# Per-tile routing in a mixture-of-experts step: selection, ranking and expert lists made as each tile's logits arrive

## The chip, the cores and the metric

The kernel runs on one core of a Trainium2 chip. The metric is the time of one execution on the device in microseconds (us), the median of three runs. All tensors are float32.

## What is computed

A prompt of 512 rows and 8 sample rows of width 1024 pass through one decoder layer: three mixers side by side (a short convolution, a gated MLP over chunks, forgetting attention), an output projection with residual add, and then the part that is changed, a hierarchical mixture of experts with 4 groups of 8 experts:

```python
def hier_moe(h, w_grp, b_grp, w_rt, b_rt, w_gate, w_up, w_down):
    grp_prob = softmax(h @ w_grp + b_grp)
    p_g, g_idx = top_k(grp_prob, 1)
    exp_logits = (h @ w_rt + b_rt) of that group
    p_e, e_idx = top_k(softmax(exp_logits), TOP_K)      # TOP_K = 2
    w = p_g * p_e / sum(p_e)
    # per expert e: act = silu(h @ w_gate[e]) * (h @ w_up[e]) * gate;  y += act @ w_down[e]
x = x + hier_moe(rmsnorm(x, g_ffn), ...)
x = x + (p_i @ w_ple) * sigmoid(rmsnorm(x, g_ple) @ w_ple_gate)
```

A final RMSNorm follows. Each row uses 2 of 32 experts; each expert has three matrices of 2 MB (1024x512, 1024x512, 512x1024).

## The kernel before, in words

The 520 rows are five tiles: tiles 0 to 3 have 128 prompt rows each, tile 4 (`QT`) has the 8 sample rows. The five engines run instruction streams written out by hand; they meet at semaphores, and each engine takes its own instructions strictly in the order written. `step(...)` on DVE issues an instruction and waits for its end; `tell(s)` raises a semaphore.

**The output projection and the second norm.** PE computes for each prompt tile t two halves of 512 columns, `mix_half(t, 0)` and `mix_half(t, 1)` (L1487). DVE adds them into x, `add_half(t, n)` (L2149). ACT squares the row (`second_norm`, L1041), POOL takes the power -1/2 (L760), DVE scales the row to `h2n` (L2170), ACT stores it to DRAM for the later gather (`store_h2`, L1045). `h2n` has two buffers. The sample rows come last: `sample_sums` on PE (L473) into four groups of partitions, three copies by ACT (`copy_parts`, L479), three adds by DVE (`add_sample`, L2159 to L2162), then the same norm.

**Logits.** `route(t)` on PE transposes a tile (L1501), waits for ACT to copy it out of PSUM (`copy_h2T`, L1053), and multiplies by the router's 36 columns (L1507); DVE adds the bias (`take_logits`, L2176). PE's order is mix 0, mix 1, route 0, mix 2, route 1, mix 3, route 2, the transposes of the per-layer input (`p01`, `p23`, `p4`, L1573), sample product, route 3, `embed(0)`, route 4, `embed(1)`. `embed(t)` (L1593) is the product of the per-layer input with `w_ple` for tile t, which is wanted only at the very end of the kernel; ACT copies it to SBUF (`copy_p_emb`, L1091). It waits for a free pair of PSUM banks.

**Routing.** Only when all five tiles' logits are there, DVE selects for all tiles at once: top group, first and second expert (L2230 to L2247), 27 instructions. PE forms running counts with a strictly triangular and an all-ones matrix (`rank`, L1604). DVE makes each pair's position in its expert's list, the overflow tables (experts that got more than 64 rows continue in spare tiles), and one-hot matrices (L2251 to L2283). PE multiplies these to lists of 50 columns (32 first tiles and 18 spare ones), `list`, 40 matmul records (L1614). DVE turns them into integer row lists (L2299 to L2307) and raises `lists_ready`. PE does `embed(2)` between `rank` and `list`, `embed(3)` and `embed(4)` after `list`, and then waits until ACT has copied all of them.

**The experts.** POOL copies a column of the list (L769) and gathers 64 rows by indirect DMA (L770). For each expert PE transposes the rows (L1628), multiplies by gate and up (L1637), ACT applies Silu (L1115), DVE multiplies (L2317), PE transposes (L1645) and multiplies by down (L1652), ACT copies out (L1121), POOL scatters (L777). SP loads the weights into two slots. Experts 0 and 1 are loaded ahead; the weights of expert 2 (`load_expert(2, 0)`, L570 and L571) go into slot 0 and are issued when the gate and up product of expert 0 has ended:

```python
sp.wait_ge(gu_full, 1)
load_expert(2, 0)
with sp.Fori(2, NE // 2) as i:
    for s in range(2):
        sp.wait_ge(gu_full, i * 2 + (s - 2))
        load_expert(i * 2 + (s - 1), 1 - s)
        sp.wait_ge(y_full, i * 2 + (s - 3))
        load_down(i * 2 + (s - 2), s)
```

After the 32 experts come the overflow tiles, if there are any, the sum over each row's two experts, the embedding gate and the final norm. In the profiled execution the overflow branch runs no tile.

## Time and profile before

| | |
|---|---|
| median of 3 runs | 1042.65 us (1041.35 to 1042.81) |
| profiled execution, its own time | 1042.36 us |
| its span, first to last instruction | 1040.6 us |
| mean granted TensorE clock | 0.909 |
| PE busy | 861.0 us (83%) |
| DVE busy | 336.7 us (32%) |
| ACT busy | 193.6 us (19%) |
| POOL busy | 261.9 us (25%) |
| bytes moved | 316.42 MB, 304 GB/s over the span |

The profiled execution lies 0.3 us below the median, so its span stands for the kernel. The busy shares are means over stages of different kinds: attention and mixers until about 330 us, projection and routing until about 443 us, the experts until about 948 us, and the last stage. TensorE's clock has two levels, 1.2 and 2.4 GHz; the profile gives it as a share of the higher, so 0.50 is the lower level throughout and values between are mixtures.

### The profile page before, as it was taken

What the parts mean: (1) busy time and instruction counts of PE and PEld (TensorE: products, weight loads), DVE (VectorE), ACT (ScalarE), POOL (GpSimd) and SP (SyncE); (2) the same over time, 40 slices, a digit from 0 to 9 for tenths busy, and PEclk for the clock granted to TensorE, in tenths of its full rate; (3) what the DMA queues carried; (4) which work ended last, traced back from release to release, by engine and by line L of the source; (5) the groups of instructions that cost most, each with busy time, mean ns of one, the idle gap of its engine ahead of it and who ended that gap; (6) DMA issues with size and microseconds to landing.
All of it is one profiled execution on the core that took longest, in us unless ns stands there. A gap on an engine that the chain in (4) does not pass through costs nothing.

```text
span 1040.6 us, 11429 instructions
## 1 busy us (share of the span) xinstructions
PE 861.0 (83%) x4225; PEld 445.4 (43%) x4225; DVE 336.7 (32%) x626; ACT 193.6 (19%) x391; POOL 261.9 (25%) x342
## 2 busy tenths in 40 slices
PE   5999888989969987688878878887787978883995
PEld 3888565746633553333333333332333333331442
DVE  5899966555434434600000000000000000011652
ACT  3110234514320012021010110101101011010431
POOL 6989785222211000112110111101111010000110
PEclk9999978998979998899988898898989789896998
DMA  9899954478984406059999999999999999996210
GB/s 307 323 337 381 341 186 162 158 277 345 357 352 173 161 21 264 9 210 411 406 417 399 408 397 405 416 397 416 413 411 417 395 409 408 427 408 273 83 41 40
DMA packets 53830, 316.42 MB, mean 304 GB/s; under 512 B 11246, under 2 KB 24110, under 8 KB 33048
## 3 DMA queue, kind: packets, MB, share of 16 engines
q1 hardware_dynamic: 34736, 233.28, 56.1%
q0 software_dynamic: 14480, 76.17, 19.1%
q10 hardware_dynamic: 4576, 6.46, 1.7%
q8 instruction: 24, 0.39, 0.2%
q14 instruction: 14, 0.11, 0.0%
HBM read 309.31 MB, written 14.82 MB: 311 GB/s over the span
## 4 chain that ended last, share of the span: by engine, by line
DMA 33%; PE 22%; DVE 2%; SPq 1%; issue 1%; ACT 0%; POOLq 0%; POOL 0%; DVEq 0%; ACTq 0%
DMA arena<-in_w_up 30%; PE psum L1637 13%; PE psum L1745 5%; DMA arena<-in_w_down 2%; PE psum L1652 1%; PE psum L1593 1%; DMA moe_rows<-arena,indices 1%; SPq L570 1%; PE psum L473 1%; SPq L599 0%; PE psum L1728 0%; DVE arena L2347 0%; PE psum L1614 0%; PE psum L1628 0%; DMA arena<-moe_rows 0%
## 5 line engine op out<-in xcount | busy, mean ns | idle before, releaser
L1637 PE MATMUL psum<-arena 128*64 128x512 f32 x1024 | 269.2, 686 | 82.9 <-DMA arena<-in_w_up 82.9
L1637 PEld LDWEIGHTS psum<-arena 128*64 128x64 f32 x1024 | 92.0, 157 | 236.0 <-issue 234.4
L2317 DVE TENSOR_TENSOR arena<-arena,psum 64x512 f32<-64x512 f32 x32 | 22.1, 692 | 381.7 <-ACT arena L1115 381.7
L1652 PE MATMUL psum<-arena 128*64 128x512 f32 x512 | 117.4, 598 | 3.8 <-DMA arena<-in_w_down 3.3
L1257 PE MATMUL psum<-arena 128*128 128x260 f32 x384 | 86.5, 388 | 0.0
L1339 PE MATMUL psum<-arena 128*128 128x260 f32 x320 | 80.1, 404 | 2.5 <-DVEq L1909 2.5
L776 POOL COPY indices<-row_list 128x1 int32 (+1 forms) x26 | 4.8, 183 | 305.4 <-ACT arena L1121 305.4
L709 POOL TENSOR_TENSOR arena<-arena 128x2048 f32<-128x2048 f32 x18 | 81.5, 4541 | 0.3
L1115 ACT ACTIVATE arena<-psum 64x512 f32<-64x512 f32 x32 | 18.9, 589 | 332.5 <-PE psum L1637 332.5
L1257 PEld LDWEIGHTS psum<-arena 128*128 128x128 f32 x384 | 73.9, 193 | 12.3 <-issue 0.8
L1817 DVE TENSOR_REDUCE arena<-arena 128x32 f32<-128x2048 f32 x32 | 72.0, 2281 | 4.6 <-POOL arena L709 3.5
L1652 PEld LDWEIGHTS psum<-arena 128*64 128x64 f32 x512 | 41.9, 139 | 72.8 <-issue 72.1
L1339 PEld LDWEIGHTS psum<-arena 128*128 128x128 f32 x320 | 61.7, 199 | 23.1 <-issue 9.4
L1487 PE MATMUL psum<-arena 128*128 128x512 f32 x128 | 59.1, 619 | 1.1 <-DVE arena L2149 1.1
L777 POOL DMA_INDIRECT moe_rows<-arena,indices x32 | 32.7, 1023 | 95.5 <-ACT arena L1121 57.3
L1745 PE MATMUL psum<-arena 128*128 128x512 f32 x128 | 55.7, 593 | 0.0
L675 POOL DMA_INDIRECT arena<-in_cache_v,indices x32 | 32.1, 1003 | 90.6 <-PE psum L1402 81.6
L2321 DVE COPY arena<-psum 128x256 f32<-128x256 f32 x32 | 13.6, 425 | 89.6 <-PE psum L1645 89.6
L1402 PE MATMUL psum<-arena 128*32 128x256 f32 x512 | 32.5, 401 | 11.5 <-DMA arena<-in_cache_v,indices 11.3
L1487 PEld LDWEIGHTS psum<-arena 128*128 128x128 f32 x128 | 24.8, 198 | 31.3 <-issue 29.8
L770 POOL DMA_INDIRECT arena<-h_rows,indices x32 | 31.1, 973 | 27.3 <-POOL indices L769 25.4
L1121 ACT ACTIVATE arena<-psum 128x512 f32<-128x512 f32 x32 | 19.1, 597 | 97.2 <-PE psum L1652 97.2
(329 smaller groups left out, 855.9 us busy)
## 6 DMA issues: line engine op xcount, KB each, us to landing
arena<-in_w_down SPq DMA_DIRECT2D x32, 2048.0 KB, 25.3
arena<-in_w_gate SPq DMA_DIRECT2D x31, 2048.0 KB, 18.0
arena<-in_w_up SPq DMA_DIRECT2D x31, 2048.0 KB, 22.7
arena<-in_w_in SPq DMA_DIRECT2D x11, 1024.0 KB
arena<-in_x_prompt SPq DMA_DIRECT2D x8, 512.0 KB, 6.7
arena<-in_w_ple_gate SPq DMA_DIRECT2D x1, 4096.0 KB, 25.9
arena<-moe_rows SPq DMA_DIRECT2D x4, 1024.0 KB, 8.0
out<-arena ACTq DMA_DIRECT2D x8, 256.0 KB
```

Of the source, the lines that this page charges most:

```text
L675: pool.indirect_dma_start(ring[s], None, caches[cache], bass.IndirectOffsetOnAxis(ap=chunk_ids[:, n:n + 1], axis=0)).then_inc(kv_in[s], 16)
L709: pool.tensor_tensor(r, r, q_rep, ALU.mult).then_inc(kmul, 1)
L770: pool.indirect_dma_start(h_rows[s][0:SLOTS, :], None, h2_dram, bass.IndirectOffsetOnAxis(ap=tok_ix[s][0:SLOTS, 0:1], axis=0), bounds_chec ...
L777: return pool.indirect_dma_start(moe_dram, bass.IndirectOffsetOnAxis(ap=row_ix[s][:, 0:1], axis=0), y_rows[s], None, bounds_check=2 * PAIR ...
L1257: last = mm(psum[:, 2 * q + half, 0:HALF], w_ring[s][:, k, q * P:(q + 1) * P], hT[:, k, half * HALF:(half + 1) * HALF], start=(k == 0), st ...
L1339: last = mm(bank(4 + half)[:, 0:HALF], w_ring[g % 2][:, k, q * P:(q + 1) * P], hT[:, k, half * HALF:(half + 1) * HALF], start=(k == 0), st ...
L1402: ins = mm(out[32 * g:32 * (g + 1), 0:WA], p[:, k * HC + 4 * half:k * HC + 4 * half + 4, :], v[:, k * WC + half * WA:k * WC + (half + 1) * ...
L1487: last = mm(mix_bank(t, n, g), heads, w_out[:, W_OUT_AT[k], n * BANK:(n + 1) * BANK], start=(k == NORMS[g][0]), stop=(k == NORMS[g][-1]))
L1637: last = mm(bank(s)[m * SLOTS:(m + 1) * SLOTS, :], hgT[s][:, k, :], w_gu[s][m][:, k, :], start=(k == 0), stop=(k == DC - 1))
L1652: last = mm(bank(6 + s)[n * SLOTS:(n + 1) * SLOTS, :], actT[s][:, k, :], w_dn[s][:, k, n * BANK:(n + 1) * BANK], start=(k == 0), stop=(k = ...
L1745: last = mm(bank(2 * (i % 2) + n), xT[i % 2][:, k, :], w_gate_ple[:, k, n * BANK:(n + 1) * BANK], start=(k == 0), stop=(k == DC - 1))
L1817: v.tensor_reduce(scores[:, n * KEYS * HC:(n + 1) * KEYS * HC], ring[SLOT[n]].rearrange("p (a d) -> p a d", d=HD), AX.X, ALU.add).then_inc ...
```

## The change

The routing is taken apart by tile. The sample tile goes ahead of prompt tile 3 (`TURN = (0, 1, 2, QT, 3)`), with its product into a PSUM fill of its own (`os`) after route 1, and `h2n` gets a third buffer. After each tile's logits DVE selects its two experts (`top_two`), PE ranks its rows (`rank_rows`, against the running sum of earlier tiles), DVE makes positions and one-hot slots (`place_rows`), and PE accumulates the lists of the 32 first tiles in a PSUM bank (`list_rows`). The overflow tables, the weights of the pairs and the spare lists move behind the first experts (`overflow`, `overflow_lists`, `count_rows`, `list_over`, `route_exps`). DVE writes the lists straight to integers.

```diff
+TURN = (0, 1, 2, QT, 3)
+POS = {t: n for n, t in enumerate(TURN)}
+H2_BUF = {0: 0, 1: 1, 2: 0, QT: 1, 3: 2}
...
@@ sync
-            sp.wait_ge(wo_full, 2 * QT + 1)
+            sp.wait_ge(wo_full, 2 * QT)
             load_expert(1, 1)
...
@@ gpsimd
             for c in range(RING):
                 gather(0, c)
+            pool.wait_ge(lists_ready, 2)
             for c in range(RING):
                 move_rows(0, c)
...
@@ scalar
-            for t in range(QT):
...
+            second_norm(1)
...
+            store_h2(1)
+            copy_h2T(1)
+            second_norm(2)
+            store_h2(2)
             second_norm(QT)
             store_h2(QT)
+            copy_h2T(2)
+            second_norm(3)
             copy_h2T(QT)
+            for name, t0, n in (("p01", 0, 2), ("p23", 2, 2), ("p4", 4, 1)):
...
+            store_h2(3)
+            copy_h2T(3)
 
             copy_p_emb(0)
             copy_p_emb(1)
-            act.wait_ge(route_exp_in, 1)
-            act.activation(eg, eg, ACT.Exp).then_inc(route_exp_out, 1)
-            act.wait_ge(route_exp_in, 2)
-            act.activation(r5[4], r5[4], ACT.Exp).then_inc(route_exp_out, 1)
...
             for e in range(LEAD):
                 expert(0, e)
+                if e == 2:
+                    route_exps()
...
@@ tensor
+            def rank_rows(t):
+                name = f"rank{t}"
+                wait_free(pe, name)
+                pe.wait_ge(route_op, ROUTE_AT[f"top{t}"])
+                last = mm(fill(name)[:, 0:NE], strict, chosen[:, t, :], start=True, stop=(POS[t] == 0))
+                if POS[t]:
+                    last = mm(fill(name)[:, 0:NE], ones, earlier[:, POS[t] - 1, :], start=False, stop=True)
+                done(last, name)
+            def list_rows(t):
+                pe.wait_ge(route_op, ROUTE_AT[f"place{t}"])
+                for c in range(2):
+                    for half in range(2):
+                        last = mm(bank(7)[half * SLOTS:(half + 1) * SLOTS, 0:2 * NE], slot_main[:, 2 * t + c, :], hits[:, 2 * t + c, :],
+                                  start=(t == 0 and c == 0), stop=(t == 3 and c == 1), skip_group_check=True)
+                if t == 3:
+                    last.then_inc(list_full, 1)
...
             route(1)
+            wait_free(pe, "os")
+            pe.wait_ge(mixs_ready, 2)
+            done(sample_sums(mm, fill("os"), mixS, w_out, order=W_OUT_AT), "os")
+            rank_rows(0)
             mix_half(3, 0)
+            route(2)
+            rank_rows(1)
             mix_half(3, 1)
-            route(2)
+            rank_rows(2)
+            route(QT)
...
-            sample_sums(mm, bank(3), mixS, w_out, order=W_OUT_AT).then_inc(wo_full, 1)
-            route(3)
...
+            transpose_h2(3)
             embed(0)
-            route(QT)
+            route_logits(3)
             embed(1)
-            wait_free(pe, "rank")
...
+            rank_rows(QT)
+            for t in (0, 1, 2):
+                list_rows(t)
             embed(2)
-            wait_free(pe, "list")
...
+            rank_rows(3)
+            list_rows(QT)
+            list_rows(3)
             embed(3)
             embed(4)
...
             for e in range(LEAD):
                 expert(0, e)
+                if e == 0:
+                    count_rows()
+                if e == 2:
+                    list_over()
...
@@ vector
             take_logits(0)
+            top_two(0)
...
             add_half(2, 1)
             second_norm(2)
             take_logits(1)
+            top_two(1)
+            add_sample()
+            place_rows(0)
+            second_norm(QT)
             add_half(3, 0)
+            take_logits(2)
+            top_two(2)
+            place_rows(1)
             add_half(3, 1)
+            place_rows(2)
+            take_logits(QT)
             second_norm(3)
-            take_logits(2)
-            add_sample()
-            second_norm(QT)
+            top_two(QT)
             take_logits(3)
-            take_logits(QT)
+            top_two(3)
+            place_rows(QT)
+            place_rows(3)
+            dve.wait_ge(list_full, 1)
+            listed = bank(7)[:, 0:2 * NE]
+            step(v.tensor_scalar(no_row, listed[:, 0:NE], 0.0, float(4 * PAIRS), ALU.is_equal, ALU.mult))
+            step(v.tensor_tensor(tok_list[:, 0:NE], listed[:, NE:], no_row, ALU.add))
+            tell(lists_ready)
...
             for e in range(LEAD):
                 activate(0, e)
+                if e == 1:
+                    overflow()
+                if e == 3:
+                    overflow_lists()
```

`top_two(t)` has 17 `step` instructions on 4 to 64 columns and one more, `count_up(t)`, except for tile 3; the choice is told to PE after the 15th. `place_rows(t)` waits for `rank{t}` and has four:

```python
def place_rows(t):
    wait_full(dve, f"rank{t}")
    for c in range(2):
        n = 2 * t + c
        step(v.tensor_tensor_reduce(out=cand, in0=fill(f"rank{t}")[:, 0:NE], in1=e_one[:, n, :], ..., accum_out=r_pos[:, n:n + 1]))
    dve.nop().then_inc(free_of(f"rank{t}"), 1)
    for c in range(2):
        n = 2 * t + c
        step(v.tensor_scalar(slot_main[:, n, :], iota, r_pos[:, n:n + 1], None, ALU.is_equal))
    tell(route_op)
```

`overflow()` holds 22 DVE instructions, in the main those that stood at L2231, L2244 and from L2258 to L2297; `overflow_lists()` has 9, `count_rows()` one product, `list_over()` 20 products (40 records, as `list` had) of 36 columns, `route_exps()` the two exponentials, on ACT after the Silu of expert 2.

## Rows read from the trace of the kernel before

**Rows 1.** The page, 40 slices of 26 us: the DMA row.

```profile
DMA  9899954478984406059999999999999999996210
```

**Rows 2.** Window of the expert stage: engines in the page's order, clock, DMA, GB/s.

```profile
518.00:582.00 64.00, 53.09 (x240) 21.17 (x238) 4.47 (x8) 7.13 (x12) 9.51 (x16) 0.87 1.01 412
```

**Rows 3.** The chain that ended last: start us, us, what.

```profile
434.46 7.42 PE psum L1593 x16
...
441.90 1.02 ACT arena L1091
...
445.95 8.36 PE psum L1637 x32
...
454.70 13.80 DMA arena<-in_w_up
```

**Rows 4.** Timeline of PE: start, us, line, operation, tiles, count [idle before].

```profile
371.21 13.98 PE L1487 MATMUL psum<-arena 128*128 128x512 f32 x32
385.03 1.04 PE L1501 MATMUL psum<-arena 128*128 128x128 f32 x8
386.96 1.95 PE L1507 MATMUL psum<-arena 128*128 128x36 f32 x16 [0.90 <-ACTq L1058]
...
392.54 5.99 PE L473 MATMUL psum<-arena 128*8 128x512 f32 x32
...
408.81 0.68 PE L1507 MATMUL psum<-arena 128*8 128x36 f32 x16 [0.45 <-ACTq L1058]
...
418.40 1.40 PE L1604 MATMUL psum<-arena 128*128 128x160 f32 x4 [5.28 <-DVEq L1757]
...
430.86 3.60 PE L1614 MATMUL psum<-arena 128*64 128x100 f32 x40 [6.83 <-DVEq L1757]
```

**Rows 5.** Timeline of DVE.

```profile
367.70 2.32 DVE L2149 SCALAR_TENSOR_TENSOR arena<-psum,arena 128x512 f32<-128x512 f32 x3 [4.54 <-PE psum L1487]
...
389.74 1.28 DVE L2170 SCALAR_TENSOR_TENSOR arena<-arena 128x1024 f32<-128x1024 f32 x1 [2.18 <-POOL arena L760]
...
403.07 1.21 DVE L2162 TENSOR_TENSOR arena<-arena 8x1024 f32<-8x1024 f32 x1
...
409.82 0.18 DVE L2230 TENSOR_REDUCE arena<-arena 128x5 f32<-128x20 f32 x1
...
412.26 0.32 DVE L2238 TENSOR_REDUCE arena<-arena 128x5 f32<-128x160 f32 x1
...
421.90 0.42 DVE L2258 TENSOR_TENSOR arena<-arena 128x256 f32<-128x256 f32 x1
...
433.68 0.18 DVE L2297 CAST over_i<-arena 128x17 int32<-128x17 f32 x1
```

**Rows 6.** Timeline of ACT.

```profile
387.65 1.06 ACT L1041 ACTIVATE arena<-arena 128x1024 f32<-128x1024 f32 x1 [0.90 <-DVE arena L2149]
...
446.61 1.28 ACT L1115 ACT_TABLE_LOAD   x1
```

**Rows 7.** Timeline of POOL.

```profile
389.16 0.54 POOL L760 TENSOR_TENSOR arena<-arena 128x1 f32<-128x1 f32 x1
...
436.53 0.18 POOL L769 COPY indices<-tok_list 64x1 int32<-64x1 int32 x1 [30.18 <-DVEq L2308]
```

**Rows 8.** DMA queues, 436 to 446 us, 40 slices.

```profile
DMA  0000000000000751000009420000422000004730
```

**Rows 9.** Windows of 4 us, columns as in the second group.

```profile
388.00:392.00 4.00, 2.19 (x17) 1.85 (x16) 1.39 (x2) 1.40 (x3) 0.74 (x2) 0.82 0.00 0
392.00:396.00 4.00, 4.00 (x24) 0.96 (x26) 0.00 (x0) 0.67 (x2) 0.00 (x0) 0.50 0.34 135
```

**Rows 10.** Timeline near the end, the same sample product at the full clock.

```profile
967.88 1.90 PE L473 MATMUL psum<-arena 128*8 128x512 f32 x16
```

**Rows 11.** Timeline of PE, the products of expert 4.

```profile
495.00 7.09 PE L1637 MATMUL psum<-arena 128*64 128x512 f32 x32 [3.31 <-DMA arena<-in_w_up]
```

**Rows 12.** Timeline of SP, the weights of expert 5.

```profile
487.42 0.33 SPq L570 DMA_DIRECT2D arena<-in_w_gate  x1
```

More of the change, by code:

```diff
@@ L170, in build @@
         mix_sc = at(c2 + 4 * SEQ + 2 * DC * NB, 4, NB)
-        h2n = [at(region_c + (2 + s) * D, D) for s in range(2)]
+        h2n = [at(region_c + (2 + s) * D, D) for s in range(3)]
         squares = at(c2, 4, SEQ)
@@ L286, in build @@
-        chosen = small(TILES, NE)
-        prod_r = small(2 * TILES, NE)
-        rank = small(TILES, NE)
+        gcand = small(NG)
+        masked, m2, cand = small(NE), small(NE), small(NE)
+        g_top, l_one, l_two, share = (small(TILES) for _ in range(4))
+        l_top = (l_one, l_two)
+        gap = l_two
+        first = small(1)
+        e_one = small(2 * TILES, NE)
+        chosen, earlier = small(TILES, NE), small(TILES, NE)
+        hits = small(2 * TILES, 2 * NE)
+        r_pos = small(2 * TILES)
@@ L289, in build @@
+        slot_main = small(2 * TILES, SLOTS)
+        no_row, row_f = small(NE), small(NE)
+        assert small_top[0] <= small0 + P + 2 * PAGE * HC + 4 * TILES * HC
+        small_top[0] = small0 + P + 2 * PAGE * HC + 4 * TILES * HC
+        eg = small(TILES, NG)
+        g_sum = small(TILES)
         cmp8 = small(NE, QMAX)
         tiles_over, over_end, over_base = small(NE), small(NE), small(NE)
[L291 to L292 removed]
@@ L1082, in _ @@
-            act.wait_ge(h2_stored[0], 32)
+            second_norm(0)
+            act.wait_ge(mixs_ready, 1)
+            step(act.activation(squares_s[:, 0:4, :], mix_ab[:, :, SEQ:NT], ACT.Square))
+            act.activation(squares_s[:, 4:8, :], mix_sc, ACT.Square).then_inc(sq_ready, 1)
+            store_h2(0)
+            copy_h2T(0)
+            second_norm(1)
+            assert stored[0] == OUTS
+            act.wait_ge(out_act, 16 * stored[0])
+            act.dma_start(w_ple_sb, a["w_ple"][0].rearrange("(k p) n -> p k n", p=P)).then_inc(ple_in, 16)
@@ L1620, in _, with count_rows, list_over @@
             pe.wait_ge(pe_free, TILES)
-            for name in ("list", "rank"):
+            for name in ("rank4", "rank3"):
                 pe.wait_ge(free_of(name), AT[name][1] + 1)
+            def count_rows():
+                pe.wait_ge(route_op, ROUTE_AT["counted"])
+                mm(bank(3)[:, 0:NE], ones, earlier[:, TILES - 1, :], start=True, stop=True).then_inc(list_full, 1)
+            def list_over():
+                pe.wait_ge(route_op, ROUTE_AT["over"])
+                for n in range(2 * TILES):
+                    for half in range(2):
+                        last = mm(bank(2)[half * SLOTS:(half + 1) * SLOTS, 0:2 * SPARE], slot_over[:, n, :],
+                                  tile_over[:, n, :, :].rearrange("p a b -> p (a b)"),
+                                  start=(n == 0), stop=(n == 2 * TILES - 1), skip_group_check=True)
+                last.then_inc(list_full, 1)
             def rows_T(rows, signal):
@@ new lines, in count_up @@
+            def count_up(t):
+                if POS[t]:
+                    step(v.tensor_tensor(earlier[:, POS[t], :], earlier[:, POS[t] - 1, :], chosen[:, t, :], ALU.add))
+                else:
+                    step(v.tensor_copy(earlier[:, 0, :], chosen[:, t, :]))
+            def place_rows(t):
+                wait_full(dve, f"rank{t}")
+                for c in range(2):
+                    n = 2 * t + c
+                    step(v.tensor_tensor_reduce(out=cand, in0=fill(f"rank{t}")[:, 0:NE], in1=e_one[:, n, :], scale=1.0, scalar=0.0,
+                                                op0=ALU.mult, op1=ALU.add, accum_out=r_pos[:, n:n + 1]))
+                dve.nop().then_inc(free_of(f"rank{t}"), 1)
+                for c in range(2):
+                    n = 2 * t + c
+                    step(v.tensor_scalar(slot_main[:, n, :], iota, r_pos[:, n:n + 1], None, ALU.is_equal))
+                tell(route_op)
@@ L2254, in _ @@
-            for t in range(1, TILES):
-                step(v.tensor_tensor(masked[:, t, :], masked[:, t, :], masked[:, t - 1, :], ALU.add))
-            step(v.tensor_tensor(rank[:, 1:TILES, :], rank[:, 1:TILES, :], masked[:, 0:QT, :], ALU.add))
-            count = masked[:, QT, :]
-            step(v.tensor_tensor(cmp8, inner(count, QMAX), outer(steps, NE), ALU.is_gt))
-            step(v.tensor_reduce(tiles_over, cmp8, AX.X, ALU.add))
-            step(v.tensor_tensor_scan(over_end, ones[:, 0:NE], tiles_over, 0.0, ALU.mult, ALU.add))
```

312 lines of the change are left out of this document (149 added, 163 removed).

## Prediction

> **What bounds the kernel now.** The page comes first, its DMA row over time [rows 1]. From slice 18 to slice 35, 468 to 936 us, the queues are full, while slices 14 and 16, 364 to 390 and 416 to 442, are empty. A window inside that stretch shows DMA at 1.01 of its share and 412 GB/s while PE works 53 of 64 us [rows 2]; the seven other windows of the stage read alike. So the expert stage is a stream of weights. Its length is set by bytes, and the end of the kernel moves with the moment at which the stream can start.
>
> The chain of waits says what that moment is [rows 3]. The weights of expert 2 are issued when expert 0's gate and up product ends at 454.3. That product follows from the transposes of the gathered rows, which start at 442.9 when ACT has copied the last `embed`, which follows PE's last two `embed` products, which follow the lists at 434.46. Everything ahead of 442.9 is therefore worth its full length, as long as something else does not start the experts later.
>
> PE's own timeline [rows 4] shows what the stretch from 371 us is made of: work, and idle time before `rank` (5.28 us) and before `list` (6.83 us) while DVE selects and builds tables [rows 5], plus pieces under 2 us. The change does the selection beside PE's mixes and puts the tables later. The question is how tight PE's work can then be packed.
>
> **The new schedule, worked out.** I walk it from 371.21, where the old mix 3 started and where the new kernel starts the sample product. Ahead of that only `top_two(0)` is new, 18 instructions on DVE. A DVE instruction on 20 columns takes 0.18 [rows 5] and the next starts 0.21 after it, so 18 cost 3.8 us; they delay the sample factors, which the new sample product wants at 371, some 10 us after they are ready. Cost nothing.
>
> 1. Sample product: 5.99 before, but in a window at half clock [rows 4, 9]; 16 records take 1.90 at full clock [rows 10], 32 take 3.8. It now follows dense work, so 3.8: 375.0. Rank 0 is 2 records; four wider ones took 1.40 [rows 4], so 0.3 to 0.4: 375.3.
> 2. Mix(3,0), half of 13.98: 382.3. Transposes of tile 2, 1.04: 383.3.
> 3. ACT must copy them, but its order has `store_h2(4)` ahead, which waits for DVE. DVE: tile 1's sum ends at 370.0 [rows 5], the norm follows 4.5 later and ends at 373.5, `take_logits` and `top_two(1)` end at 377.6, `add_sample` 1.21 + 2 x 0.70 = 2.6: 380.2. From the Square to the scaling took 389.74 - 387.65 = 2.1 [rows 5 to 7], the scaling 1.28: 383.7. The DMA issue on ACT 0.3, the copy until the logits' start 1.3: 385.4. PE idles 2.1 us here, and DVE holds back `add_half(3, 0)` by 1.4, which nobody wants yet. Logits 1.8: 387.2.
> 4. Rank 1 0.4, mix(3,1) 7.0: 394.6. Sum into x 2.3: 397.0. POOL's power and ACT's Square end at 399.1, but DVE first takes the sample logits. Their second transpose waits for the bank of rank 2, which `place_rows(2)` frees at 397.5; copy until 398.8 behind ACT's Square; product 0.7 [rows 4]; bias 0.2; then the norm of tile 3, 1.28: 401.0. The transposes of tile 3 wait for the banks of the per-layer input: 402.3.
> 5. PE from there without a wait: embed 0 3.7 (7.42 for two [rows 3]), logits 3 1.8, embed 1 3.7, rank 4 0.4, lists of three tiles (24 records at 3.60 / 40 = 0.09 [rows 4]) 2.2, embed 2 3.7, rank 3 0.4: 418.2. `top_two(3)` ran from 408.0 to 411.7 beside embed 1.
> 6. `place_rows(3)`, four instructions and two hand-overs, 1.1 with tile 4's list beneath it; the last list 0.7: 420.0. Embed 3 and 4, 7.4, ACT's copy 1.1: 428.5.
> 7. Clock. The wait-ridden stretch from 394.6 to 402.3 has about 3 us of work in 7.7. Before, a stretch with 2.19 us busy in 4 was followed by a window at 0.50, the lower of the two levels [rows 9]. Embed 0 would then start at half clock, up to 3.7 more. I take half of it, 1.8: 430.3.
>
> Gain at this point 442.9 - 430.3 = 12.6. Expert 0's transposes and product (8.36, partly at the lower level) I leave as they are.
>
> **Does anything else start the experts later?** The lists reach POOL 0.5 after step 6's list, 422.3 with the clock term. Before, POOL began at 436.53 and the first gather's data had moved by 440.2 [rows 7, 8], 3.7 later: 426.0, 4.3 us ahead of the embeds' end. The weights of expert 1 are issued at about 394.7 and took 16 us, so 411. SP's queue has nothing else ahead of them. The rows' stores wait for nothing new.
>
> **What moved behind.** The table work before spans 421.90 to 433.86 on DVE [rows 5], 12.0 with its waits; the 22 instructions of `overflow` are about 8.2 of it. They start after expert 1's copy and end about when expert 2's product is wanted; that product may be 1 us late, and PE has a down product of 3.6 us there before it wants the result. PE gets 40 list records after expert 2, 3.6 us, ahead of expert 3's product, so the weights of expert 5 (issued at 487.42 [rows 12]) go out 3.6 later. At that time expert 4's weights were still under way; they ended at 495.0 [rows 11], 7.6 later. The stream does not run dry: cost nothing, with 4 us of cover, and if it were gone 3.6. ACT loads two tables, 1.28 each [rows 6], and has 7 us free between the copy of expert 1 and the Silu of expert 3. The lower list conversions go from 6 instructions to 2 on the path, which step 6 has. Overflow itself is not run.
>
> Sum against the profiled execution: 1042.36 - 12.6 = 1029.8, and 0.3 more against the median of the runs: **1030.0 us**.
>
> **Bounds.** What the trace does not show: `tensor_tensor_reduce` (from 0.18, as a small operation, to 0.32, as 160 columns took, so 0.2 to 0.6 in all on the path); the instructions with three operands, the same bounds: with 0.35 in place of 0.21 `top_two(1)` puts 2.5 on step 3 and place 0.5; the clock term, 0 to 3.7; expert 0's product, 7.09 at full clock, 1.3 less. The gain runs from 12.6 - 1.9 - 3.0 - 0.6 = 7.1 to 12.6 + 1.8 + 1.3 = 15.7.
>
> **Rivals.**
> - *The clock stays up* from the sample product to expert 0: no term 7, expert 0 at 7.09: gain 15.7, 1027. For it speaks that PE has two embeds and logits in a row; against it the gaps of step 4.
> - *DVE becomes the bound.* Per tile 18 + 4 instructions, some 110 in all, nearly all at the fixed cost of a small one: 0.18 for 20 columns against 0.32 for 160 [rows 5]. If they cost 0.35 each and hand-overs 0.1, steps 3, 4 and 6 stretch by 2.5 + 1 + 2, and with all of term 7 by 7.4: gain 5 to 8, 1035 to 1037. Against it: PE has embeds to do while tile 3 is selected. The Trainium skill ("VectorE: DVE Perf Modes", section on the TRN2 errata) speaks against the change here: a fixed extra latency is paid by each instruction, so many small tiles pay it each time. By its formula, (N + 151) / 0.96 ns, 32 columns would take an estimated 0.19 us, and the trace agrees with 0.18 at 20 columns.
> - *The moved work runs the stream dry* (the other side): DVE's 12.0, the 3.6 of lists and two table loads end to end in experts 1 to 3 are 18.2 against 12.6, 5.6 slower, 1048. It decides only if the three stand one behind another on the path and no weights are outstanding; the trace shows 7.6 us outstanding [rows 11, 12].
> - *No change*: something outside fixes the stream's start, such as expert 1's weights. They would have to come 19 us later than worked out.
>
> **How the numbers follow.** Forecast (gain 9 to 15, 1027.6 to 1033.6) 0.68; clock up 0.12; DVE bound 0.13; dry stream 0.03; no change 0.02; 0.02 for other losses. The range takes the forecast, the clock rival and the near part of the DVE one: 1026 to 1035. Faster by over 0.2% (2.1 us, about what a measurement of this kernel can tell from no change) 0.94, within 0.2% 0.02, slower 0.04.
>
> **What would show it.** In the profile after: PE's first gathered-row transposes at 430, with an `embed` copy as what released them, not the gather; POOL's first list copy near 422; expert 2's weights issued near 441.6; in the chain nothing of `top_two` behind the rank of tile 2; the windows of the expert stage as before in DMA share and GB/s, also in the first 60 us; the expert stage as long as before. The prediction is wrong if PE waits for DVE between 375 and 394 for more than 3 us, if the DMA share falls below 0.95 in experts 3 to 6, or if the last stage starts at another distance from expert 2's weights than before.

## The result, and the profile after

The change made the kernel faster: 1032.5 us, median of 13 runs (1026.2 to 1037.2), against 1042.2 us before on the same chips (1039.2 to 1044.0). The ratio is 0.9914, 95% interval 0.9892 to 0.9936, a gain of 9.7 us in medians. The forecast was 1030.0, with a range of 1026 to 1035. One profiled execution stands for each kernel below; where the text says that a profile took so long, it is that one execution. The profiled execution of the changed kernel took 1035.3 us, 7.0 less than the profiled one before and near the slow end of the 13.

The page of the changed kernel, its slices (25.8 us each), beside [rows 1]:

```profile
PE   5999888988969988899877878798877869783994
...
PEclk9999978998979996989998898988999898997998
DMA  9899954378994225269999999999999999997111
```

The expert stage is the same stream as before, full from slice 18 on. In PEclk slice 15 (388 to 413 us), in the middle of the routing, is at 0.6.

Where the time of the profiled execution went is read from the chain that ended last, the part that answers to [rows 3]:

```profile
425.39 7.18 PE psum L1644 x16
...
432.59 1.02 ACT arena L1108
...
433.66 1.11 PE psum L1683 x8
...
436.65 9.64 PE psum L1692 x32
...
449.77 8.17 PE psum L1692 x32
```

The first transposes of gathered rows (L1683) start at 433.66, released by the copy of the last embed (ACT, L1108), as forecast; before they started at 442.97. That is 9.3 us won, of which 1.3 are given back at once: expert 0's product (L1692) takes 9.64 where it took 8.36 [rows 3]. The weights of expert 2 go out at 446.3 against 454.3, 8.0 earlier. From SP's timelines, before and after:

```profile
454.33 0.33 SPq L570 DMA_DIRECT2D arena<-in_w_gate  x1
```

```profile
446.30 0.33 SPq L581 DMA_DIRECT2D arena<-in_w_gate  x1
```

From there to the end of the span the kernel takes 587.2 us, before 586.3. So 8.0 minus 0.9 is the 7.1 by which the spans differ.

PE's timeline of the stretch, which answers to [rows 4], and the clock and DMA of the same time in windows of 4 us (columns as in [rows 2]). In the changed kernel L484 is the sample product, L1507 a mix, L1521 the transposes and L1530 the logits of a tile, L1542 and L1544 rank, L1552 the lists, L1627 the transposes of the per-layer input and L1644 an embed:

```profile
371.43 3.62 PE L484 MATMUL psum<-arena 128*8 128x512 f32 x32
...
375.22 7.11 PE L1507 MATMUL psum<-arena 128*128 128x512 f32 x16
382.17 1.04 PE L1521 MATMUL psum<-arena 128*128 128x128 f32 x8
386.02 2.50 PE L1530 MATMUL psum<-arena 128*128 128x36 f32 x16 [2.82 <-ACTq L1075]
...
389.18 9.53 PE L1507 MATMUL psum<-arena 128*128 128x512 f32 x16
...
401.52 0.59 PE L1521 MATMUL psum<-arena 8*128 8x8 f32 x4 [2.11 <-DVEq L2285]
...
406.43 1.94 PE L1521 MATMUL psum<-arena 128*128 128x128 f32 x8 [0.47 <-ACT arena L1099]
408.16 5.07 PE L1644 MATMUL psum<-arena 128*128 128x512 f32 x8
...
418.75 0.92 PE L1552 MATMUL psum<-arena 128*64 128x64 f32 x24
...
425.32 7.23 PE L1644 MATMUL psum<-arena 128*128 128x512 f32 x16
```

```profile
382.00:386.00 4.00, 1.21 (x9) 0.80 (x8) 2.90 (x4) 1.20 (x4) 0.71 (x2) 1.00 0.06 8
386.00:390.00 4.00, 3.98 (x21) 3.66 (x22) 1.77 (x8) 0.00 (x0) 0.00 (x0) 0.65 0.02 4
390.00:394.00 4.00, 4.00 (x6) 1.69 (x5) 3.25 (x18) 0.00 (x0) 0.00 (x0) 0.50 0.00 0
394.00:398.00 4.00, 4.00 (x10) 1.71 (x9) 0.35 (x2) 0.00 (x0) 0.00 (x0) 0.99 0.00 0
398.00:402.00 4.00, 1.89 (x14) 1.40 (x12) 2.96 (x9) 0.90 (x1) 0.00 (x0) 0.86 0.54 176
402.00:406.00 4.00, 3.44 (x28) 2.83 (x27) 2.18 (x7) 1.34 (x6) 0.74 (x2) 0.50 1.03 438
406.00:410.00 4.00, 3.57 (x11) 2.57 (x12) 3.15 (x15) 1.55 (x4) 0.00 (x0) 0.50 1.06 417
...
438.00:442.00 4.00, 4.00 (x12) 1.14 (x10) 0.00 (x0) 0.58 (x1) 0.72 (x1) 0.52 0.07 19
...
458.00:462.00 4.00, 4.00 (x26) 1.53 (x23) 0.69 (x1) 1.16 (x2) 0.00 (x0) 1.00 0.75 262
```

The two waits of 2.82 and 2.11 us are where the prediction put them. What it did not foresee is the length of the work behind the first: mix(3,1) takes 9.53 us for 16 records, mix(3,0) 7.11. The windows say why. PE was busy 1.21 of 4 us from 382 on, and from 390 to 394 the granted clock is 0.50, the lower of the two levels. The second sparse piece, 398 to 402, is followed by 0.50 from 402 to 410, in which the transposes of tile 3 and embed 0 (5.07) run.

### The profile page after: what moved, and what is told of

Read it like the earlier page. It is cut to its first block, busy times and chain, and to the rows that moved or that the text cites. A ratio compares the mean times of both kernels' runs of the same rounds, so it can differ in the third digit from the quotient of the medians.

```text
span 1033.5 us, 11650 instructions
## 1 busy us (share of the span) xinstructions
PE 867.0 (84%) x4281; PEld 450.8 (44%) x4281; DVE 348.3 (34%) x710; ACT 196.0 (19%) x393; POOL 261.2 (25%) x342
## 4 chain that ended last, share of the span: by engine, by line
PE 53%; DMA 35%; DVE 5%; issue 2%; ACT 2%; POOL 2%; SPq 1%; POOLq 0%; DVEq 0%; ACTq 0%
DMA arena<-in_w_up 31%; PE psum L1692 14%; PE psum L1277 8%; PE psum L1359 7%; PE psum L1805 5%; PE psum L1507 5%; PE psum L1422 2%; PE psum L1644 2%; DMA arena<-in_w_down 1%; PE psum L1371 1%; DMA arena<-in_cache_v,indices 1%; PE psum L1401 1%; PE psum L1707 1%; PE psum L1530 1%; PE psum L1383 1%
## 5 line engine op out<-in xcount | busy, mean ns | idle before, releaser
L1692 PE MATMUL psum<-arena 128*64 128x512 f32 x1024 | 270.8, 689 | 82.3 <-DMA arena<-in_w_up 82.3
L1692 PEld LDWEIGHTS psum<-arena 128*64 128x64 f32 x1024 | 91.8, 158 | 237.3 <-issue 235.5
L1507 PE MATMUL psum<-arena 128*128 128x512 f32 x128 | 61.8, 640 | 1.1 <-DVE arena L2209 1.1
L1805 PE MATMUL psum<-arena 128*128 128x512 f32 x128 | 55.7, 593 | 0.0
L1507 PEld LDWEIGHTS psum<-arena 128*128 128x128 f32 x128 | 25.7, 206 | 32.3 <-issue 30.8
```

The costliest lines, as they stand in the source:

```text
L1507: last = mm(mix_bank(t, n, g), heads, w_out[:, W_OUT_AT[k], n * BANK:(n + 1) * BANK], start=(k == NORMS[g][0]), stop=(k == NORMS[g][-1]))
L1692: last = mm(bank(s)[m * SLOTS:(m + 1) * SLOTS, :], hgT[s][:, k, :], w_gu[s][m][:, k, :], start=(k == 0), stop=(k == DC - 1))
L1805: last = mm(bank(2 * (i % 2) + n), xT[i % 2][:, k, :], w_gate_ple[:, k, n * BANK:(n + 1) * BANK], start=(k == 0), stop=(k == DC - 1))
```

## The experiments

The experiments ran in three sets, each on one chip and in turn with the kernel before: again, fill, no_tables and order; fill_first, tables_ahead, packed and packed_fill; before_fill, twice_1, twice_3 and order_fill. Ratios can be compared across the sets, medians less well. Each ratio is to before; the change itself gave 0.9914. A profile's time is cut at three moments: the start of the sample product (of mix 3 in the kernels before), the first row transposes, and the issue of expert 2's weights. Between the first two lies what is called the stretch from here on, behind the third the stream. This is needed because the start of the stretch wandered by up to 5.7 us from profile to profile in kernels that are the same up to there:

| kernel | sample product starts | the stretch: to the first row transposes | expert 2's weights issued | the stream: from there to the end of the span | ratio, 95% interval |
|---|---|---|---|---|---|
| before | (371.2, mix 3) | 71.8 | 454.3 | 586.3 | 1 |
| the change | 371.4 | 62.2 | 446.3 | 587.2 | 0.9914 (0.9892 to 0.9936) |
| again | 374.2 | 61.4 | 445.7 | 586.0 | 0.9925 (0.9909 to 0.9941) |
| fill_first | 370.5 | 58.2 | 439.9 | 588.8 | 0.9891 (0.9864 to 0.9918) |
| fill | 368.9 | 55.3 | 434.3 | 584.1 | 0.9841 (0.9807 to 0.9874) |
| no_tables | 371.9 | 61.5 | 443.4 | 586.3 | 0.9899 (0.9875 to 0.9924) |
| tables_ahead | 374.0 | 66.2 | 451.9 | 584.1 | 0.9956 (0.9933 to 0.9979) |
| twice_1 | 374.4 | 64.8 | 449.2 | 586.6 | 0.9958 (0.9940 to 0.9977) |
| twice_3 | 370.5 | 62.7 | 443.2 | 583.6 | 0.9920 (0.9888 to 0.9952) |
| order | 373.0 | 54.9 | 437.9 | 586.9 | 0.9826 (0.9804 to 0.9849) |
| packed | 372.0 | 53.6 | 435.6 | 587.2 | 0.9848 (0.9817 to 0.9879) |
| packed_fill | 368.7 | 52.2 | 431.2 | 586.8 | 0.9819 (0.9791 to 0.9848) |
| order_fill | 372.9 | 52.3 | 435.2 | 584.1 | 0.9806 (0.9777 to 0.9834) |
| before_fill | (372.8, mix 3) | 68.7 | 451.5 | 585.8 | 0.9967 (0.9949 to 0.9985) |

The row transposes came at 433.7 where the prediction had 430.3, and the time was 2.5 us over the forecast in the median, 5.5 in the profile. The theories on where this goes: **clock**, PE's waits are followed by work at the lower clock; and its rivals, **stream** (the moved tables drain the weight stream) and **DVE** (its selections are the bound).

### again: the change once more

No edit.

> The changed kernel once more, on the chip of the three others, as their yardstick. Clock theory: times spread over 1026 to 1037 as before, median near 1032.5, because the half-clock stretches between 386 and 454 us (0.50 in 390 to 394, 402 to 410 and near 440 us in the profile) come and go from run to run. Rival, the stream theory: the spread comes from the 500 us of weight stream; then the profile of this run has the same first 446 us as the one at hand and another length behind them.

1033.4 us, 1032.2 to 1034.1. The spread of the first 13 did not come back in these six. Its profile shows the same pair of low stretches (0.50 in 390 to 394 and in 406 to 410) but expert 0 at 7.09 us, so which products fall into the lower clock does change from execution to execution. The stream took 586.0. Half of the clock theory's expectation held, the spread did not.

### fill: unused products in PE's waits

```diff
+            def keep_busy(b, n, added):
+                pe.wait_ge(wo_free, added)
+                for _ in range(n):
+                    mm(bank(b), ident, tri, start=True, stop=True)
...
-            route(2)
+            transpose_h2(2)
+            keep_busy(3, 3, 6)
+            route_logits(2)
             rank_rows(1)
             mix_half(3, 1)
             rank_rows(2)
+            keep_busy(0, 2, 2 * QT)
             route(QT)
...
             embed(3)
             embed(4)
+            keep_busy(6, 1, 2 * QT + 1)
```

> The changed kernel with six products of ident by tri added, whose results nobody reads, in PE's waits: three after the transposes of tile 2 (a wait of 2.8 us), two ahead of the sample tile's transposes (2.1 us), one behind the last embed (1.1 us). Nothing else is changed. Clock theory: mix(3,1) takes 7.0 instead of 9.5, embed 0 3.7 instead of 5.1, expert 0 about 8.4 instead of 9.6, expert 1 7.1 instead of 8.2; 5 to 7 us faster than the changed kernel, 1026 or less, and with less spread. Rival, the work of PE alone is the bound: the added products cost what they overhang, 0 to 1 us slower.

1023.7 us, ratio 0.9841. `keep_busy` multiplies two constant matrices into a PSUM bank that is free at the time; each product of 512 columns is two records (L1560). The windows of this kernel (columns as above), which has the same reads and writes besides six products nobody reads:

```profile
382.00:386.00 4.00, 3.76 (x25) 2.73 (x24) 2.39 (x6) 1.08 (x2) 0.00 (x0) 1.00 0.08 12
...
390.00:394.00 4.00, 4.00 (x13) 1.97 (x12) 2.14 (x9) 0.00 (x0) 0.00 (x0) 1.00 0.17 33
394.00:398.00 4.00, 2.99 (x32) 2.00 (x31) 2.44 (x10) 1.32 (x4) 0.74 (x2) 1.00 0.89 336
...
402.00:406.00 4.00, 4.00 (x23) 2.81 (x22) 1.51 (x8) 1.02 (x1) 0.00 (x0) 1.00 0.92 373
```

```profile
380.55 2.74 PE L1560 MATMUL psum<-arena 128*128 128x512 f32 x6
...
385.75 7.11 PE L1507 MATMUL psum<-arena 128*128 128x512 f32 x16
...
393.07 1.96 PE L1560 MATMUL psum<-arena 128*128 128x512 f32 x4
...
400.25 3.60 PE L1652 MATMUL psum<-arena 128*128 128x512 f32 x8
...
427.13 7.09 PE L1701 MATMUL psum<-arena 128*64 128x512 f32 x32
```

mix(3,1) is at 7.11, embed 0 at 3.60, expert 0 at 7.09, and no window from 362 to 462 us is under 1.00. From the sample product to the row transposes it takes 55.3 us instead of 61.4 to 62.2. That is 6 to 7 us, as the clock theory had it; nothing but PE's waits was changed, and the first wait ends when it ended before (logits 2 start 14.6 us after the sample product in both kernels). The DMA share here is 0.92 to 1.04 from 398 to 410 at a clock of 1.00, so the queues' activity, which in the changed kernel coincides with the second low stretch, does not account for it. The median fell by 9.7 against again; the 3 us more are not explained by the filling: this profile also began the stretch 5.3 us earlier than again's, ahead of any edit, and the six runs reach from 1019 to 1031.

### fill_first: only the first wait

```diff
-            route(2)
+            transpose_h2(2)
+            keep_busy(3, 3, 6)
+            route_logits(2)
             rank_rows(1)
```

The two other `keep_busy` of fill are not in it.

> The changed kernel with only the first of the three fillings of the run fill: three unused products after the transposes of tile 2, in the 2.8 us in which PE waits for ACT. Clock theory: logits 2 takes 1.9 instead of 2.5 to 3.6 and mix(3,1) 7.0 instead of 8.4 to 9.5, so 3 to 5 us faster than the changed kernel (about 0.988 of before), and the rest of the 6 to 7 us that the full filling gained in the stretch comes from the second wait. Rival: the gain of fill came from chance in where the stage began, and this run is the changed kernel's equal, 0.992.

1029.6 us, ratio 0.9891, between the two. The profile shows mix(3,1) at 7.11 again, and embed 0 at 5.63 behind the second wait, which was left open:

```profile
387.28 7.11 PE L1507 MATMUL psum<-arena 128*128 128x512 f32 x16
...
397.21 0.41 PE L1521 MATMUL psum<-arena 8*128 8x8 f32 x4 [2.11 <-DVEq L2292]
...
402.60 5.63 PE L1651 MATMUL psum<-arena 128*128 128x512 f32 x8
```

The first wait costs 3 to 4 us of clock and the second some 3: each is told by its own filling (61.4 to 62.2, then 58.2, then 55.3), in one profile each. The ratio's interval overlaps that of the changed kernel, so this step rests on the stretch and its rows, not on the time alone.

### no_tables: the moved work left out

```diff
             for e in range(LEAD):
                 expert(0, e)
-                if e == 0:
-                    count_rows()
-                if e == 2:
-                    list_over()
```

and on DVE in `overflow()` and `overflow_lists()`:

```diff
-                step(v.tensor_tensor(cmp8, inner(bank(3)[:, 0:NE], QMAX), outer(steps, NE), ALU.is_gt))
...
-                step(v.tensor_copy(over_f[:, OVER:OVER + 1], over_end[:, NE - 1:NE]))
+                step(v.memset(over_f, 0.0))
                 step(v.tensor_copy(over_i[:, 0:OVER + 1], over_f))
...
-                dve.wait_ge(list_full, 3)
...
-                step(v.tensor_tensor(row_list[:, NE:], over_row, no_over, ALU.add))
```

That is 19 instructions for one, and four more in the second. This kernel leaves out the tables of the overflow tiles and their lists; the exponentials and the weights of the pairs, which moved too, stay.

> The changed kernel without the overflow tables and spare lists that stand among the first experts: 17 instructions on DVE in overflow, 4 in overflow_lists, one count product and 20 list products on PE are left out; the number of overflow tiles is set to zero, the exponentials and shares stay. Theory of the prediction: the stream has 4 us of cover, so at most 0.5 us faster than the changed kernel. Rival: the moved work drains the stream, 2 to 5 us faster, with the DMA share at 1.0 where it was 0.94 in 458 to 470 us.

1031.5 us, ratio 0.9899; the stream takes 586.3, the same as in again (586.0). In medians it is 1.9 us faster than again, and the intervals overlap. That is more than the 0.5 expected and at the low edge of the 2 to 5 of the stream theory; the profile puts none of it into the stage where the tables stand. The DMA share from 11.9 to 23.8 us behind the issue of expert 2's weights is 1.01 here where it was 0.94 in the changed kernel, which is what the stream theory asked for; but it is 1.01 in again as well, with the tables in place. The stream theory as the cause of the missing time falls; a cost of up to 2 us is not excluded.

### tables_ahead: the moved work put back

```diff
             list_rows(QT)
             list_rows(3)
+            count_rows()
             embed(3)
             embed(4)
...
+            list_over()
             rows_step(0, 0)
             for e in range(LEAD):
                 expert(0, e)
-                if e == 0:
-                    count_rows()
-                if e == 2:
-                    list_over()
...
+            overflow()
+            overflow_lists()
             upper = slice(SLOTS, 2 * SLOTS)
```

The last lines are DVE's, ahead of its first `activate`; on ACT the exponentials stand behind `copy_p_emb(2)`, and `count_rows` uses a bank that is free there.

> The changed kernel with one of its parts undone: the overflow tables, spare lists and exponentials stand ahead of the first expert again, the count product behind the last list product, the spare lists on PE behind embed 4. The per-tile selection, ranking and listing stay. Theory: DVE's tables (8.3 us from about 427) run beside embeds 3 and 4, so PE waits 2 to 3 us and does 1.4 us of lists: rows_T 4 us later than in the changed kernel, but also a table load on ACT less behind it; in all 3 to 4 us slower than the changed kernel, 0.995 to 0.996 of before. Rival: the tables' move was the main part of the change's gain; then at least 8 us slower, no faster than before.

1037.8 us, ratio 0.9956: some 4 us slower than the changed kernel (0.0031 to 0.0042 in ratio). The stretch grew by 4.8 us over again's, about as expected, and the stream gave some back. Of the 4.8, PE's rows put 1.5 into a further wait for DVE, 1.4 into the spare lists, and 1.7 into the lower clock once more: embeds 3 and 4 take 8.91 for 7.23 behind the wait. The per-tile routing alone, with the tables still ahead, is worth 3 us by the medians and 4.6 by the ratio, and moving the tables about as much again.

### twice_1 and twice_3: a selection done twice

```diff
+                for _ in range(2 if t == 1 else 1):       # twice_3: t == 3
                     top = slice(t, t + 1)
                     group = logits[:, t, 0:NG]
...
```

The loop holds the 14 selecting instructions of `top_two`.

> The changed kernel with the selection of tile 1 done twice (14 more DVE instructions, 3.2 us). Theory of the prediction's step 3: this selection stands ahead of add_sample on DVE and so on the path to logits 2 through the store on ACT; PE's wait there grows from 2.8 to 6 us, and with the clock it costs 3 to 6 us, 0.995 to 0.998. Rival, DVE is nowhere near the path: nothing, 0.992.

> The changed kernel with the selection of tile 3 done twice (14 more DVE instructions, 3.2 us). Rank 3 on PE comes 4.3 us after DVE told the choice, because embed 2 stands between, so by the PE theory this costs nothing, 0.992. Rival, DVE is the bound after logits 3: 3 us, 0.995.

twice_1: 1037.6 us, 0.9958, 3 to 4 us slower than the changed kernel; twice_3: 1032.8 us, 0.9920, no different. So 3.2 us on DVE cost 3 to 4 us in tile 1's selection and next to nothing in tile 3's, where the only trace of them on PE is a wait of 0.48 us ahead of the sample tile's list. In twice_1 the transposes of tile 2 themselves must wait (`place_rows(0)` frees their bank late) and logits 2 start 3.98 us after them; in twice_3 rank 3 starts without a wait:

```profile
387.69 0.66 PE L1521 MATMUL psum<-arena 128*128 128x128 f32 x4 [1.70 <-DVEq L2286]
392.33 3.60 PE L1530 MATMUL psum<-arena 128*128 128x36 f32 x16 [3.98 <-ACTq L1075]
```

```profile
418.63 3.70 PE L1644 MATMUL psum<-arena 128*128 128x512 f32 x8
422.17 0.30 PE L1542 MATMUL psum<-arena 128*128 128x32 f32 x2
...
423.18 0.45 PE L1552 MATMUL psum<-arena 128*64 128x64 f32 x8 [0.48 <-DVEq L1817]
```

DVE is neither the bound nor free: its place in the order decides.

### order: the two products of tile 3 kept together

```diff
             rank_rows(0)
             mix_half(3, 0)
-            route(2)
             rank_rows(1)
             mix_half(3, 1)
-            rank_rows(2)
+            route(2)
             route(QT)
...
             embed(0)
+            rank_rows(2)
             route_logits(3)
...
             add_half(3, 0)
-            take_logits(2)
-            top_two(2)
             place_rows(1)
             add_half(3, 1)
-            place_rows(2)
-            take_logits(QT)
+            take_logits(2)
             second_norm(3)
+            take_logits(QT)
+            top_two(2)
             top_two(QT)
+            place_rows(2)
             take_logits(3)
```

> The changed kernel with the two products of tile 3 back to back (mix(3,1) right after mix(3,0) and rank 1, route 2 behind both) and DVE's order to match (place 1, then the second sum of tile 3, then logits 2, the norm of tile 3, the sample logits, and only then the selections of tiles 2 and 4). Theory: in the changed kernel PE's order and waits, not DVE's selection, hold the stretch: the 2.8 us wait before logits 2 goes, mix(3,1) runs at the full clock and ends near 389 instead of 398.6, the norm of tile 3 is 9 us earlier, and rows_T starts near 424 instead of 433.7: 8 to 10 us faster than the changed kernel, about 1023. Rival, DVE is the bound: the two selections now stand one behind the other after 395 and the third starts near 404, so the rows start at 429 or later and the gain is 4 or less.

1024.9 us, ratio 0.9826: 8.6 us faster than again, measured on the same chip. The stretch takes 54.9. The wait of 2.8 us is down to 0.90 without any filling and mix(3,1) takes 7.11. DVE's selections in a row cost nothing: rank 3 on PE does not wait for them. Embed 0 still takes 4.87, behind the sparse transposes.

```profile
384.09 7.11 PE L1507 MATMUL psum<-arena 128*128 128x512 f32 x16
...
392.97 2.25 PE L1530 MATMUL psum<-arena 128*128 128x36 f32 x16 [0.90 <-ACTq L1075]
...
402.14 4.87 PE L1643 MATMUL psum<-arena 128*128 128x512 f32 x8
```

### packed and packed_fill: short pieces moved into the dense part

In packed the transposes of the per-layer input stand around mix(3,1), embed 0 ahead of tile 3's transposes, embed 1 ahead of logits 3, and the first row transposes ahead of the wait for ACT's embed copies. ACT's copies follow, and DVE does `place_rows(1)` and the second sum of tile 3 one step earlier. PE's order, as it stands in the kernel:

```python
            mix_half(3, 0)
            rank_rows(1)
            pe.wait_ge(ple_in, 48)
            transpose_p_emb("p01", (0, 1))
            mix_half(3, 1)
            transpose_p_emb("p23", (2, 3))
            transpose_h2(2)
            transpose_p_emb("p4", (4,))
            route_logits(2)
            route(QT)
...
            embed(0)
            transpose_h2(3)
            rank_rows(2)
            embed(1)
            route_logits(3)
...
            rows_step(0, 0)
            pe.wait_ge(pe_free, TILES)
```

packed_fill adds to packed:

```diff
+            keep_busy(0, 1, 2 * QT)
             route_logits(2)
...
             list_rows(QT)
+            keep_busy(6, 1, 2 * QT + 1)
             list_rows(3)
...
             rows_step(0, 0)
+            keep_busy(6, 1, 2 * QT + 1)
             pe.wait_ge(pe_free, TILES)
```

> The run order, and in addition the transposes of the per-layer input between the products of tile 3 and behind them, embed 0 ahead of the transposes of tile 3, embed 1 ahead of logits 3, and PE's first transposes of gathered rows no longer behind ACT's copies of the embeds. No filling. Theory (the sparse stretch from 391 to 402 us, where PE has many short pieces, goes at the lower clock and is emptied of waits): rows_T 5 us earlier than in order, 50 us after the sample product's start where order has 54.9, 1019 to 1021 in all. Rival: DVE's three selections in a row are the bound now; then rank 3 waits for top_two(3) by over 2 us and nothing is won over order, 1025.

> The run packed with three unused products, one in each of PE's waits that are left: ahead of logits 2, ahead of the last list product, between the first two transposes of gathered rows. Clock theory: no window under 1.00 between 370 and 450 us, 1 to 3 us faster than packed, about 1018. Rival: packed has no gap long enough to cost clock; equal to it.

packed: 1025.1 us, 0.9848, nothing won over order; packed_fill: 1021.5 us, 0.9819, not told from either by its interval. The stretch of packed is 53.6 us, only 1.3 shorter than order's. The rival had the result right and the cause wrong, for PE waits for DVE only 0.46 and 0.86 us, ahead of the last lists. PE's rows say what happened: embed 0 takes 5.40 in its new place and embeds 3 and 4 take 8.93 instead of 7.23.

```profile
383.52 7.03 PE L1511 MATMUL psum<-arena 128*128 128x512 f32 x16
...
395.06 0.77 PE L1525 MATMUL psum<-arena 8*128 8x8 f32 x8
...
396.89 5.40 PE L1650 MATMUL psum<-arena 128*128 128x512 f32 x8
...
416.71 8.93 PE L1650 MATMUL psum<-arena 128*128 128x512 f32 x16
```

packed_fill mends the last two (7.23) but not embed 0, which stays at 5.40 behind some five us of short records, in spite of the product ahead of logits 2. What decides this is open: embeds 3 and 4 took 7.23 in the changed kernel too, behind a wait of 0.90 and no filling.

### order_fill: the waits of order filled as well

The edit, on top of order's:

```diff
-            route(2)
+            transpose_h2(2)
+            keep_busy(0, 1, 2 * QT)
+            route_logits(2)
             route(QT)
...
             list_rows(QT)
+            keep_busy(6, 1, 2 * QT + 1)
             list_rows(3)
             embed(3)
             embed(4)
+            keep_busy(6, 1, 2 * QT + 1)
...
+                if isinstance(i, int) and i == 0 and c == 0:
+                    keep_busy(6, 1, 2 * QT + 1)
                 pe.wait_ge(act_ready, num(i, c + 1))
```

The last one fills expert 0's wait for DVE's product.

> The run order with four unused products, one ahead of logits 2, one ahead of the last list product, one behind embed 4, one in expert 0 while PE waits for DVE. Clock theory: embed 0 at 3.7 instead of 4.9, expert 1 at 7.1 instead of 8.8 so that the stream does not run dry there, 3 to 5 us faster than order, 1020 or less, the fastest of all. Rival: the lower clock in the sparse stretch from 391 to 402 us comes from short pieces, not from waits, and one product does not cure it; equal to order, 1024.

1021.1 us, 1020.1 to 1022.3, ratio 0.9806 (0.9777 to 0.9834), the lowest measured; its interval overlaps those of order and packed_fill, so that it is faster than order is not shown. Embed 0 is at 3.60, experts 0 and 1 both at 7.09. The one product ahead of logits 2 did not keep the clock up, though: the lower level comes later and is left earlier (0.50 from 398 to 402 in order), and what runs in it are short pieces instead of embed 0.

```profile
394.00:398.00 4.00, 3.56 (x37) 3.29 (x36) 2.26 (x7) 1.01 (x4) 0.74 (x2) 0.70 1.02 434
398.00:402.00 4.00, 3.49 (x19) 2.38 (x18) 3.33 (x17) 2.35 (x5) 0.00 (x0) 0.87 1.02 430
```

```profile
400.62 3.60 PE L1650 MATMUL psum<-arena 128*128 128x512 f32 x8
```

### before_fill: the same filling in the kernel before

```diff
+            keep_busy(6, 5, 2 * QT)
             wait_free(pe, "rank")
...
+            keep_busy(6, 7, 2 * QT)
             wait_free(pe, "list")
...
             embed(3)
             embed(4)
+            keep_busy(6, 1, 2 * QT)
```

> The kernel before the change with 13 unused products in PE's waits: 5 ahead of rank (a wait of 5.28 us), 7 ahead of list (6.83 us), 1 behind the last embed (1.07 us). Clock theory: the kernel before pays the lower clock too, in embed 2 (4.4 instead of 3.7), the lists and expert 0 (8.4 instead of 7.1): 2 to 3 us faster, 0.997 to 0.998, much less than the 9 us that filling gave the changed kernel, so that the change's own gain at a full clock is 15 us and more. Rival: filling helps both alike; then before gains 8 us, 0.992.

1038.3 us, ratio 0.9967 (0.9949 to 0.9985). Expert 0 takes 7.09, embed 2 3.60, the 40 list records 1.96 instead of 3.60 [rows 4]. The kernel before lost about 3 us to the clock (2.7 by the medians, 3.4 by the ratio). With the waits filled in both, the change is worth 1038.3 - 1023.7 = 14.6 us by the medians, across two chips, and 13 us by the two ratios; some 3 us of it are fill's unexplained ones.

## Why the prediction was right, step by step

**The bound.** Right, within 5 us. The time follows the moment at which expert 2's weights go out, in all fourteen profiles of the table: from there to the end they take 583.6 to 588.8 us.

**Steps 1 and 2.** Right to 0.3 us: sample product 3.62 at full clock, and mix(3,0) ends at 382.3 as forecast, from a start 0.2 later.

**Step 3.** The path was right (logits 2 wait for the store on ACT, behind DVE's sample tile), and twice_1 shows that it is one. Its wait was 2.82 us for 2.1, just under the 3 us that the prediction named as a sign of being wrong. (The prediction's "4.5 later" for the norm counts from the start of tile 1's sum, not from its end; the time it gives, 373.5, is right.) The instructions on DVE follow each other by 0.23 rather than 0.21; logits 2 start at 386.0, not 385.4.

**Step 7, the clock, is the term that was mis-sized.** It had 1.8 us, all of it at embed 0, behind the second wait. It gave nothing to the first wait, 2.8 us at 383, though the row it used (a stretch with 2.19 us busy in 4, then 0.50 [rows 9]) fits that one as well: 1.21 in 4. Measured behind the first wait: mix(3,1) 9.5 for 7.1, logits 2 2.5 for 1.9, two ranks 0.6 each for 0.4, 3.4 in all. Behind the second: the transposes of tile 3 1.9 for 1.0, and embed 0 5.1, where step 5 and the term had 5.5. Filling both waits won 6 to 7 us, against the 1.8 of the term. "Expert 0 left as it is" was also off in the profiled execution, 9.6 for 8.4. Expert 1's slow product (8.2) delayed expert 3's weights to 458.15, and the DMA share was 0.75 in 458 to 462; that fits the 0.9 us lost in the stream. The other profiles say the same: where expert 1's product took 8.2 to 8.8 (the change, fill_first, order, packed, packed_fill), the DMA share from 11.9 to 23.8 us behind expert 2's issue is 0.91 to 0.96 and the stream takes 586.8 to 588.8; in the nine others it took 7.09, the share is 1.00 to 1.03 and the stream takes 583.6 to 586.6. No run changed that product alone. In again, twice_1, twice_3 and no_tables, filled nowhere, expert 0 took 7.09, so that is one of the things that differ from run to run.

**Steps 5 and 6.** The order was right and the lists were cheaper: 24 records took 0.92 us, not 2.2, because the row that priced them (40 records in 3.60) was itself at the lower clock. With the clock term the row transposes were put at 430.3 and came at 433.7: embed 0 started 5.9 us late (408.2 for 402.3), and 2.5 of it were made up behind.

**How much of it was luck.** Some. In the profile 3.4 us to the row transposes, 1.3 in expert 0 and 0.9 in the stream make up the 5.5 by which it missed 1029.8, so that as a single execution it lies on the upper edge of the range; the median run is 2.8 us faster. The clock term was 4 to 5 us too small, and other terms were too large: with the clock up the prediction had 1027, and fill measured 1023.7.

**What moved behind.** Right in its mechanism: DVE's block ran from 462.5 to 470.9 beside expert 2's product, PE's 40 records took 1.36, and the stream was not drained there (share 1.01 from 470 to 488; 0.98 over the first 64 us, before 0.99).

**The rivals.** "The clock stays up" is what fill makes of the kernel: it was put at 1027 and measured at 1023.7. "DVE becomes the bound" fell with twice_3 and order, though twice_1 shows DVE on the path in one place. "The stream runs dry" fell with no_tables, as to its size. The Trainium skill ("VectorE: DVE Perf Modes", the section on the TRN2 errata) says that many small tiles pay a fixed cost for each tile. The trace agrees with the figure estimated from its formula, 0.19 us for 32 columns in an addition; instructions with a scalar operand for each row took 0.22 to 0.25. The price was paid, 17 or 18 instructions for each of five tiles, but most of it beside PE's work: twice_1 shows the tile where it was paid in full.

**Left open.** Why the stretch starts between 368.7 and 374.4 us in profiles of kernels that are the same up to there. The granted clock between 300 and 370 us goes with it (0.91 in the two earliest, 0.85 in the two latest), but nothing was tried there. Also open are whether no_tables' 1.9 us are real, and why fill gained some 3 us more than its stretch.

## What to carry to other kernels

Ahead of a stream that fills the DMA queues a microsecond saved is one off the total, here to within the 5 us by which the stream itself varies. When waits are moved, price what comes after them too: here waits of 2.8 and 2.1 us on TensorE cost about 3 us each in the products behind them. Two cures worked, each alone: the order (the two dense products back to back, the short pieces behind them) and unused products in the wait. A row that prices an operation should be read together with the clock of its window.

## What was unexpected

- Work that nobody reads made the kernel faster: six products of 512 columns, 5.8 us of PE time (2.74 + 1.96 + 1.12), for 6 to 7 us of the stretch.
- In the changed kernel the lower clock comes after the sparse piece rather than in it: the window of the wait (382 to 386) reads 1.00, that of dense products from 390 to 394 reads 0.50.
- What short records do to the clock these runs do not settle. In packed PE was busy 4.95 of the 6 us from 390 to 396 with transposes of 8 and 128 columns and products of 36, and embed 0 behind them took 5.40 for 3.60. In fill it was busy 4.44 of the 6 us from 394 to 400 with the last of two unused products and then the same kinds of pieces, and embed 0 took 3.60 at a clock of 1.00.
